# Attention output stored before its norm, the norm's factor worked out in the second projection, and a KS times r product done in ten slices

## The reference

```python
def rms_norm(t, g):
    return t * rsqrt(mean(t * t, axis=-1) + 1e-6) * g

def short_conv_mixer(z, conv_w, g_out):          # 256 columns out
    b, cg, h = split(z, 3)
    u = cg * h
    y = conv_w[0] * shift_prev(u) + conv_w[1] * u + conv_w[2] * shift_next(u)
    return rms_norm(b * y, g_out)

def mla_mixer(...):                              # 256 columns out
    y = softmax_attend(q, k, v)                  # 4 heads of 64
    return rms_norm(merge_heads(y), g_out_mla)

def rwkv_out(y, r, v, k_sum, ...):
    ...
    y = y + sum(r * k_sum * r_k) * v             # k_sum * r is "KS times r"
```

## Time and profile before

| | value |
|---|---|
| median of three runs | 4340.51 us (4336.57 to 4342.79) |
| profiled execution, and its span | 4334.16 us, 4332.3 us |
| mean granted TensorE clock | 0.932 |
| busy in the span | PE 89%, DVE 33%, ACT 19%, POOL 11% |
| attention, layer 0 and layer 1 | 181.6 to 388.3 us, 2484.5 to 2675.8 us |
| token-major jobs of the projection | 493.2 to 634.8 us, 2761.4 to 2889.4 us |
| first of the four scans | 920.2 to 1008.6 us |

### The profile page before, as it was taken

The page is one execution under the profiler, slowest core; times in us unless marked ns, Lnnn a source line. Parts: engine busy times, 40 slices in busy tenths (PEclk is TensorE's granted clock), DMA queues, the critical chain, the costliest instruction groups (busy, mean ns, idle before and its releaser), DMA issues. The chain is left out here.

```text
span 4332.3 us, 59839 instructions
## 1 busy us (share of the span) xinstructions
PE 3847.7 (89%) x25466; PEld 2160.1 (50%) x25466; DVE 1408.7 (33%) x3018; ACT 813.0 (19%) x1840; POOL 457.9 (11%) x697
## 2 busy tenths in 40 slices
PE   6898999677897699999997898998697895999998
PEld 4555445466744344444443654444486552444444
DVE  3452112687634200000002443113777533101010
ACT  3342010344311000000002343011434210000000
POOL 1100000321200000000001100000331100000000
PEclk8999999788998899999998899999698997999999
DMA  6201110200174666666663001110100328888884
GB/s 229 107 1 30 54 54 1 74 13 18 41 281 189 246 247 246 247 250 246 245 240 116 25 4 30 56 46 26 59 4 18 109 83 308 303 322 304 321 304 158
DMA packets 190040, 612.73 MB, mean 141 GB/s; under 512 B 34472, under 2 KB 42920, under 8 KB 183120
## 3 DMA queue, kind: packets, MB, share of 16 engines
q1 hardware_dynamic: 169232, 542.30, 33.4%
q0 software_dynamic: 20544, 66.60, 5.2%
HBM read 561.07 MB, written 47.79 MB: 141 GB/s over the span
## 5 line engine op out<-in xcount | busy, mean ns | idle before, releaser
L2506 PE MATMUL ps<-moe_w,e_xT 128*128 128x512 f32 x1024 | 450.8, 598 | 0.8 <-ACT e_xT L2568 0.8
L2543 PE MATMUL ps<-moe_w,e_hT 128*128 128x512 f32 x1024 | 445.9, 593 | 6.1 <-ACT e_hT L2587 6.1
L2513 PE MATMUL ps<-moe_w,e_xT 128*128 128x512 f32 x1024 | 444.7, 592 | 0.0
L526 PE MATMUL ps<-hT,p_w 128*128 128x512 f32 (+1 forms) x880 | 327.1, 534 | 0.0
L2506 PEld LDWEIGHTS ps<-moe_w,e_xT 128*128 128x128 f32 x1024 | 194.9, 192 | 246.8 <-issue 245.6
L2513 PEld LDWEIGHTS ps<-moe_w,e_xT 128*128 128x128 f32 x1024 | 194.6, 190 | 244.9 <-issue 244.9
L2609 DVE TENSOR_TENSOR e_hid<-e_hid,ps 128x512 f32<-128x512 f32 x64 | 43.9, 686 | 838.1 <-PE ps L2513 838.1
L2543 PEld LDWEIGHTS ps<-moe_w,e_hT 128*128 128x128 f32 x1024 | 192.0, 190 | 239.0 <-issue 239.0
L2190 PE MATMUL ps<-M,yT 128*128 128x512 f32 x576 | 259.7, 606 | 9.8 <-DMA o_br<-in_b_router_dram 6.3
L526 PEld LDWEIGHTS ps<-hT,p_w 128*128 128x128 f32 x880 | 167.2, 190 | 159.3 <-issue 153.1
L1006 PE MATMUL ps<-M 96*128 96x512 f32 (+1 forms) x400 | 184.1, 546 | 5.9 <-ACT a_pr L1130 3.9
(11 more groups left out here) (357 smaller groups left out, 5522.4 us busy)
## 6 DMA issues: line engine op xcount, KB each, us to landing
moe_w<-in_w_gate_dram SPq DMA_DIRECT2D x64, 2048.0 KB, 12.9
moe_w<-in_w_up_dram SPq DMA_DIRECT2D x64, 2048.0 KB, 10.7
moe_w<-in_w_down_dram SPq DMA_DIRECT2D x64, 2048.0 KB, 17.0
o_mod_w<-in_w_ada_dram SPq DMA_DIRECT2D x24, 1024.0 KB, 10.3
m_mod_w<-in_w_ada_dram SPq DMA_DIRECT2D x16, 1024.0 KB, 5.9
p_w<-in_w_in_dram SPq DMA_DIRECT2D x6, 2048.0 KB, 7.9
r_z<-z_rows SPq DMA_DIRECT2D x20, 512.0 KB, 3.4
z_rows<-p_zo POOLq DMA_DIRECT2D x36, 256.0 KB, 2.3
```

The lines of the kernel that those rows point to most:

```text
L526: ins = nc.tensor.matmul(ps[:, j % NB, 0:tw], w[n % RW][:, k, m * P:(m + 1) * P], hT[:, k, t0:t0 + tw], start=(k == 0), stop=(k == KT - 1))
L2506: ins = nc.tensor.matmul(ps[:, c, :], xT[:, 4 * half + k], wp[:, k, c * 512:(c + 1) * 512], start=(half == 0 and k == 0), stop=(half == 1 ...
L2513: ins = nc.tensor.matmul(ps[:, 2 + c, :], xT[:, 4 * half + k], wp[:, k, c * 512:(c + 1) * 512], start=(half == 0 and k == 0), stop=(half = ...
L2543: ins = nc.tensor.matmul(ps[:, 6 + c, :], hT2[:, 4 * half + k], wp[:, k, c * 512:(c + 1) * 512], start=(half == 0 and k == 0), stop=(half ...
```

## The change

In `stage_mla_attend` the norm is taken out: no squares, no variance, no power, no normed rows `on`, no gain, no program for POOL. `mixed` turns `o` itself, one step earlier (steps 10, 14, 18 and so on), ACT copies both halves in one instruction, and the wait for `ye` goes from `outputs` to `values`. In `stage_project` the norm is done on the columns: squares of `yT[:, 2:4]` on ACT at job `tok0 + 2`, sums by the matrix of ones on PE after jobs `tok0 + 4` and `tok0 + 6`, variance on DVE at the jobs behind them, a second Ln and a second Exp at `tok0 + 16`, two more products on DVE at `tok0 + 19`, and one more small load on SP. In `stage_rwkv_scan` POOL's one product of 1280 columns becomes one of 128 columns at the end of each of its ten steps.

```diff
@@ stage_project
+    MSQ_AT, MSUM_AT, MSUM2_AT = 2, 4, 6
+    y0, n_ctx = (0, 1) if need_ctx else (CTX, 0)
...
-                def squares_sum(s, b):
+                def squares_sum(r, s, b):
                     t0, tw = SPANS[s]
                     for i in range(2):
-                        ins = nc.tensor.matmul(ps[:, b, 0:tw], g.ones, M[:, 4 + i, t0:t0 + tw], start=(i == 0), stop=(i == 1))
+                        ins = nc.tensor.matmul(ps[:, b, 0:tw], g.ones, M[:, r + i, t0:t0 + tw], start=(i == 0), stop=(i == 1))
...
+                    if j == tok0 + MSUM_AT:
+                        pe.wait_ge(*sqd.at(1))
+                        if need_ctx:
+                            squares_sum(6, 0, 6)
+                        squares_sum(6, 1, 7)
+                    if j == tok0 + MSUM2_AT:
+                        pe.wait_ge(*vard.at(1))
+                        squares_sum(6, 2, 6)
...
+                    if j == tok0 + MSQ_AT:
+                        nc.scalar.activation(M[:, 6:8, y0:T], yT[:, 2:4, y0:T], ACT.Square).then_inc(*sqd.up())
...
-                        nc.scalar.activation(M[:, 0], M[:, 0], ACT.Ln).then_inc(*lnd.up())
+                        nc.scalar.activation(M[:, 0], M[:, 0], ACT.Ln)
+                        nc.scalar.activation(M[:, 6, y0:T], M[:, 6, y0:T], ACT.Ln).then_inc(*lnd.up())
                         act.wait_ge(*lnd.at(1))
-                        nc.scalar.activation(M[:, 0], M[:, 0], ACT.Exp, scale=-0.5).then_inc(*g.rq.up())
+                        nc.scalar.activation(M[:, 0], M[:, 0], ACT.Exp, scale=-0.5)
+                        nc.scalar.activation(M[:, 6, y0:T], M[:, 6, y0:T], ACT.Exp, scale=-0.5).then_inc(*g.rq.up())
...
+                    if j == tok0 + MSUM_AT + 1:
+                        variance(6, (0, 1) if need_ctx else (1,), n_ctx)
+                    if j == tok0 + MSUM2_AT + 1:
+                        variance(6, (2,), n_ctx)
...
                         for i in range(2):
-                            ins = nc.vector.scalar_tensor_tensor(yT[:, i], M[:, 2 + i], go[:, i:i + 1], M[:, 0], ALU.mult, ALU.mult)
-                            link(ins)
+                            nc.vector.scalar_tensor_tensor(yT[:, 2 + i, y0:T], yT[:, 2 + i, y0:T], gm[:, i:i + 1], M[:, 6, y0:T],
+                                                           ALU.mult, ALU.mult)
+                            link(nc.vector.scalar_tensor_tensor(yT[:, i], M[:, 2 + i], go[:, i:i + 1], M[:, 0], ALU.mult, ALU.mult))
@@ stage_mla_attend, PE
-                    if k >= 4:
-                        pe.wait_ge(*ye.at((k - 2) // 2))
+                    if k >= 3:
+                        pe.wait_ge(*ye.at((k - 1) // 2))
...
                 def outputs(k):
                     pe.wait_ge(*ote.at(k + 1))
-                    if k >= 3:
-                        pe.wait_ge(*ye.at((k - 1) // 2))
...
                 def mixed(n):
-                    pe.wait_ge(*ond.at(n + 1))
-                    pe.wait_ge(*ote.at(min(2 * n + 4, 2 * NQ)))
+                    pe.wait_ge(*od.at(min(2 * n + 3, 2 * NQ)))
+                    pe.wait_ge(*ote.at(min(2 * n + 3, 2 * NQ)))
                     for i in range(2):
-                        ins = nc.tensor.transpose(ps[:, OB, (2 + i) * P:(3 + i) * P], on[:, n % 2, i * P:(i + 1) * P], g.ident)
+                        ins = nc.tensor.transpose(ps[:, OB, (2 + i) * P:(3 + i) * P], o[:, n % 2, i * P:(i + 1) * P], g.ident)
...
-                        if i == 1 and s >= 11 and s % 4 == 3:
-                            mixed((s - 11) // 4)
+                        if i == 1 and s >= 10 and s % 4 == 2:
+                            mixed((s - 10) // 4)
@@ stage_mla_attend, ACT
-                    if s >= 11 and s % 4 == 3:
-                        n = (s - 11) // 4
+                    if s >= 10 and s % 4 == 2:
+                        n = (s - 10) // 4
                         act.wait_ge(*ytr.at(n + 1))
                         t = qtiles[n]
-                        for i in range(2):
-                            ins = nc.scalar.activation(yT[:, 2 + i, t * P:(t + 1) * P], ps[:, OB, (2 + i) * P:(3 + i) * P],
-                                                       ACT.Copy, scale=go[:, i:i + 1])
-                        ins.then_inc(*ye.up())
+                        nc.scalar.copy(yT[:, 2:4, t * P:(t + 1) * P], ps[:, OB, 2 * P:4 * P].rearrange("p (a n) -> p a n", a=2)).then_inc(*ye.up())
...
@@ stage_rwkv_scan, POOL
-                nc.gpsimd.tensor_tensor(R["KS"][p][:], R["KS"][p][:], M[:, p], ALU.mult)
+                    ts = slice(s * P, (s + 1) * P)
+                    nc.gpsimd.tensor_tensor(R["KS"][p][:, ts], R["KS"][p][:, ts], M[:, p, ts], ALU.mult)
```

More of the change, by code:

```diff
@@ L486, in wait_target @@
                 else:
-                    eng.wait_ge(*vard.at(2))
+                    eng.wait_ge(*vard.at(4))
             elif j >= tok0 + RO:
@@ L572, in conv @@
                             dve.wait_ge(*ev[1].at(tok0 // 2))
-                            dve.wait_ge(*small.at(80))
+                            dve.wait_ge(*small.at(96))
                             if not need_ctx:
@@ L973, in stage_mla_attend @@
         o = sb("o", [P, 2, GW])
-        on = sb("on", [P, 2, GW])
-        junk = sb("junk", [P, GW])
-        ss = sb("ss", [P, 2])
-        go = sb("go", [P, 2])
-        small, chain, pw_in = sg("small_in"), sg("dve_chain"), sg("rw_g")
+        chain, pw_in = sg("dve_chain"), sg("rw_g")
         sc, mxd, ex, tg = sg("at_sc"), sg("at_mx"), sg("at_ex"), sg("at_st")
         te_a, te_d, pv, ote = sg("evac_a"), sg("evac_d"), sg("at_pv"), sg("at_ote")
-        otr, od, sqd, ond, ytr, ye = sg("at_otr"), sg("at_od"), sg("sq_done"), sg("normed"), sg("transposed"), sg("at_ye")
+        otr, od, ytr, ye = sg("at_otr"), sg("at_od"), sg("transposed"), sg("at_ye")
         def turned_out(eng, n):
@@ L992, in _ @@
             def _(sp):
-                with nc.allow_non_contiguous_dma(reason="vectors into columns"):
-                    sp.dma_start(go[:], col(I["g_out_mla"][l], 2)).then_inc(*small.up(16))
                 sp.dma_start(first_weights(g), I["w_in"][l].rearrange("(k p) f -> p k f", p=P)[:, :, 0:512]).then_inc(*pw_in.up(16))
@@ L1060, in _ @@
                         outputs((s - 5) // 2)
-            @block.gpsimd
-            def _(pool):
-                for n in range(NQ):
-                    pool.wait_ge(*g.vr.at(n + 1))
-                    nc.gpsimd.tensor_tensor(ss[:, 1:2], ss[:, 1:2], g.mhalf[:, 0:1], ALU.pow).then_inc(*g.rq.up())
             def turned_copy(eng, copy, u, i, done):
@@ L1104, in _ @@
                                                 rc[:].unsqueeze(2).broadcast_to([P, 2, HD]), ALU.mult).then_inc(*od.up())
-                    if s >= 9 and s % 4 == 1 and (s - 9) // 4 < NQ:
-                        dve.wait_ge(*sqd.at((s - 9) // 4 + 1))
-                        nc.vector.tensor_scalar(ss[:, 1:2], ss[:, 0:1], 1.0 / GW, EPS, ALU.mult, ALU.add).then_inc(*g.vr.up())
             @block.scalar
             def _(act):
-                act.wait_ge(*small.at(16))
                 for s in range(NU + 8):
```

38 lines of the change are left out of this document (14 added, 24 removed).

## The result

The changed kernel took 4303.12 us (median of three runs, 4299.94 to 4311.47) where the kernel before took 4340.51. The ratio is 0.9919, with a 95% interval from 0.9894 to 0.9944: faster. The forecast was 4312.5 us with a range from 4303 to 4328, so the direction held, and the range held by 0.1 us: 37 us were gained where 28 were forecast. The profiled execution of the changed kernel is the slowest of its three (4311.47 us, span 4309.6 us, mean granted clock 0.932). The same kernel run again, in the first experiment, left a profile of 4299.62 us at a clock of 0.937. Two executions of the experiments ran far slower, one of again (18049.81 us, mean clock 0.206) and one of slices_only (7230.88 us, 0.722), and are left out of every ratio and median.

What follows compares the result with a forecast made beforehand. PE (busy 89%) bounds most stages, through waits in attention and gapless work in the projection; a chain through all engines bounds the scan. Attention -23.8, projection +7.7, scan -12.3 + 0.4: -28.0 from 4340.5 gives 4312.5 us, range 4303 to 4328.

Steps and rivals of the forecast that it cites:

- attention, layer 0: Attention in layer 0: some 13 us shorter, from 8 waits that go and the shorter end.
- attention, layer 1: Attention in layer 1: 10.6 us shorter, from 6 waits that go and the shorter end.
- added sums on TensorE: Projection: added products with the ones, all on PE's path, cost 7.7 us (2.58 + 1.72 and 1.72 + 1.72).
- scans, both layers: Scans: the long POOL product's hold on DVE goes, -12.3 us; the slices add 0.4 us.
- The waits in attention: Attention: PE's wait at `outputs` for ACT's copies goes, 1.27 us each, and `values` waits no longer in its place.
- Rival 2: Attention: the wait only moved, `values` stands for `ye` as `outputs` did; 4330 us, chance 0.10.
- the steady part: Attention before each layer's end: 14 of the 16 waits go, 14 x 1.27 = 17.8 us gained.
- The end of attention: Attention after the last `values`: the norm's chain goes, 3.0 us a layer, 6.0 us in all, bounds 4 to 7.
- rival 1: Scan: each of the 36 slices meets DVE's scaling at its start, giving the gain back; 4321 us, chance 0.14.
- rival 3: Scan: POOL's product was not what held DVE, the chain stops there anyway; 4325 us, chance 0.07.
- a better clock: Whole kernel: better clock behind shorter pauses, some 6 us, counted only in the range's lower end.
- Rival 4: Projection and attention's steady part: work in another rhythm gets a lower clock, making it slower; 4365 us, chance 0.04.

Runs made afterwards that it cites:

- again: The changed kernel run once more, unchanged: 4299.62 us, ratio 0.9906 to the kernel before.
- slices_only: The kernel before with only the scan's POOL product cut into slices, attention and projection as before: 4321.47 us, ratio 0.9965.
- attn_only: The changed kernel without the slices, the scan's POOL product in one piece as before: 4317.73 us, ratio 0.9954.
- pair_sum: The changed kernel with DVE adding the two squares tiles before the sum, one ones-product a span in both norms: 4291.54 us, ratio 0.9886.
- act_scale_after: The changed kernel with ScalarE instead of VectorE scaling the scan's state: 4296.91 us, ratio 0.9909.
- best: The changed kernel with squares tiles added on VectorE in both norms and the scan's state scaled by ScalarE: 4290.64 us, ratio 0.9889.
- act_scale_long: The kernel before, long POOL product kept, with ScalarE instead of VectorE scaling the scan's state: 4313.27 us.
- slices256: The kernel before with the scan's POOL product in slices of 256 columns, one in every second step: 4334.01 us.
- long_mid: The kernel before with the scan's one long POOL product placed at the end of step 4: 4328.27 us.
- wait_stays: The changed kernel with `mixed` one step later and the wait at `outputs` as before, the norm still in the projection: 4319.73 us.
- late_turn_slices: The kernel before with the slices, norm kept in attention, `mixed` one step later, its wait moved to `values`, gain multiplied on DVE: 4295.14 us, ratio 0.9904.

## Why the prediction was right, and where its sizes were off

To size the terms better than one execution can, I averaged the stages over the profiles of kernels with the same code in that stage: six with the changed attention (after, again, attn_only, pair_sum, act_scale_after, best), five with the old one (before, slices_only, act_scale_long, slices256, long_mid), the scans of seven kernels with the slices and of two with the long product at the end (a mean per layer).

| term | forecast | measured |
|---|---|---|
| attention, layer 0 | -13.2 | 206.5 to 192.7: -13.8 |
| attention, layer 1 | -10.6 | 188.4 to 177.5: -10.9 |
| the projection's start, both layers | none | 199.2 to 196.1: -3.1 |
| added sums on TensorE | +7.7 | +7.7 |
| scans, both layers | -12.3 + 0.4 | 2 x (229.1 to 222.35) = -13.5 |
| sum | -28.0 | -33.5 |

- **The waits in attention: right in their cause.** The distances from the start of one `values` to that of the next show it: in the pattern's even run, those with a `mixed` between them were 11.74 to 11.75 us, six times in layer 0 and five in layer 1, and are 10.47 now, 1.28 us less where 1.27 was forecast. Rival 2 has no ground: `values` waited for the copy twice, not 16 times. wait_stays shows the cause by putting the wait back.
- **The start of attention is a term that the prediction lacks.** In layer 0 the first `values` comes 6.12 to 6.13 us after the first row maximum in the profiles of all nine runs whose ACT program starts without a wait, and 7.46 to 7.80 us after it in the five that keep the wait for the gain; in layer 1 it is 15.7 to 15.9 against 17.0 (18.6 in before). That is some 3 us in both layers. It is not the norm's chain: late_turn_slices keeps the chain, has no such wait, and has the short start. Why the table load stands where it does was not tried by itself.
- **The sum of the steady part came out right partly by luck.** In layer 0 the stretch from the first row maximum to the last `values` went from 197.1 to 186.8 us, 10.3 where 8 x 1.27 = 10.2 was forecast; in layer 1 from 178.6 (2489.2 to 2667.8) to 171.2 us (2479.6 to 2650.8), 7.4 where 6 x 1.27 = 7.6 was. Taken apart, the eight waits are worth 10.2 us in layer 0 and the six 6.9 in layer 1. The earlier start adds 1.6 and 2.9 between these two executions, and a longer way from the last `values` but one to the last takes 1.3 and 2.4 back. In layer 0 that way also has a lower clock (0.89 from 350 to 366 us, in this execution and in again); in the four others with the changed attention it is 1.00 there, and the stretch is 185.0 us.
- **The end of attention: the chain went as forecast, its size depends on the clock.** From the last `values` to the projection's first product it is 8.1 to 4.8 us in layer 1 (-3.3, forecast -3.0), but 8.35 to 7.06 in layer 0 (-1.3). The term took the last `values` at its old 2.40 us. At a lower clock it took 3.8 to 4.5 us in 9 of the 12 layers with the changed attention (layer 0 of all six kernels among them) and in 3 of the 10 with the old one. What brings the low clock there isn't shown.
- **The projection's start is the other term that the prediction lacks.** The old code needed 111.4 to 112.1 us in layer 0 and 87.2 to 88.6 in layer 1, in all executions; the changed one 109.7 in four of six and 111.4 in two (attn_only and act_scale_after), and 85.5 to 85.6 in five of six and 87.3 in one. In the windows of its first 5 us in layer 0 the clock is 0.66 before (0.50 to 0.66 in the five with the old attention), 1.00 in the four short ones, 0.66 in the two long ones, and 0.53 in late_turn_slices. So the difference is the clock. It isn't a low stretch that only came earlier: attn_only has both, a last `values` of 3.96 us and a start at 0.66. Nor is the norm's chain of 2.3 us all of it: wait_stays has none, and still starts at 0.71. What goes along with the full clock is a short way from the end of the last `values` to the projection: 2.4 to 2.5 us in the six kernels, 3.4 to 3.6 in wait_stays, and 5.1 to 6.2 where the chain stands. This wasn't tried by itself, and in three of the twelve places (two layers of six kernels) the short way came with the lower clock, so the cause stays open.
- **The added sums: right,** 4.3 and 3.4 us, and so was that no wait was added on TensorE's path.
- **The scan: right in its cause, a little short in size.** The four last steps took 43.9 us and take 31.8, 12.1 us less where 12.3 was forecast. The slices cost 0.01 us in a common step and 0.22 in four steps of layer 1, some 1.2 us in all where 0.4 was taken; rival 1 describes just these four. Together that is 11 us. The mechanism is shown from three sides, by the width (slices256), by the place (long_mid), and by taking the held instruction off DVE (act_scale_long). Rival 1 falls for the other 32 steps, and rival 3 falls. The rule cited from the Trainium skill ("SBUF — State Buffer", section "Who interferes with whom") held in each of these runs, for the instructions that it calls untouched too (0.28 us inside the 2.91). The prediction retold it a little short: the page exempts instructions with at most one SBUF input only outside VectorE's two-port modes, and names `tensor_scalar` among those that can enter these. The rest of the 13.5 us, 2.6, is smaller than the scatter of the same stretch between executions (220.4 to 225.0 us a layer, the part between the two scans included).
- **What stays open** is the last part of the gain. The stages explain 33.5 us; the medians show 37 and 36, the second ratio 41. The 21 runs of the kernel before in that set lie between 4328.67 and 4354.54 us, and a straight line through their times falls by some 2.7 us for each 0.001 of mean granted clock. The changed kernel's two profiles already differ by 11.8 us. So 3 to 7 us can't be given to any stage. The prediction had a better clock (some 6 us) in its range and not in its sum. Some 3 us of that are shown, at the projection's start; the range held by 0.1 us, and the second set's median of 4299.62 lies under it, beside a lower median of the kernel before (4335.90).
- **Rival 4, slower by the clock,** did not come true: the mean clock of the changed kernel's runs is 0.932 to 0.939, that of before 0.927 to 0.937.

## What to carry to other kernels

When one engine waits for another's copy at a certain place in a repeating pattern, first move the wait and its producer by one step, to a place with slack; here that gave all of attention's 22 us, but for some 3 that came with a wait taken off ScalarE's start. Moving the work itself elsewhere has to pay for what it adds on the path of the bounding engine: 20 small products of TensorE cost 7.7 us and bought some 4. Halving all 44 such products, the convolution's own with them, by an addition on an idle engine was worth 8 us. Look at a stage's first rows as well: a wait at the head of a program can hold what needn't wait. And an instruction on an engine that is hardly used can be the one that holds a recurrence: look for a row that is ten times its usual length, and at what ran on its neighbour engine at that moment.

## What the runs showed of the hardware

- A GpSimd `tensor_tensor` between SBUF operands holds a VectorE `tensor_scalar` between SBUF operands until 0.04 to 0.05 us after its own end, for lengths of 0.46, 0.73 and 2.89 us (128, 256 and 1280 columns of float32). ScalarE's instructions (0.35 us) and VectorE's with an operand in PSUM (0.28 us) run on in the same moment.
- The same 40 products took 4.53 us at a granted clock of 0.50 (layer 0) and 2.40 us at 1.00 (layer 1), in one execution and behind the same idle time of 0.55 us. Rows that look alike can be granted either level.
- ScalarE's table load (1.28 us) ran ahead of the first row maximum where nothing was waited for at the head of its program, and behind it where the gain's load was (the rows at the start of attention).
